# Recurrence of a hybrid trunk: a chunk's values formed beside the preceding chunk's solution, response products one gap earlier, VectorE's order changed

## Reference

```python
def rwkv_scan(s0, r, w, k, v, a_vec, b_vec, reverse, emit):
    def step(s, inp):
        r_t, w_t, k_t, v_t, a_t, b_t = inp
        sa = jnp.einsum('bhvk,bhk->bhv', s, a_t)
        s = s * w_t[:, :, None, :] + sa[..., None] * b_t[:, :, None, :] + v_t[..., None] * k_t[:, :, None, :]
        y = jnp.einsum('bhvk,bhk->bhv', s, r_t) if emit else None
        return s, y
...
for layer in range(2):
    m = token_mixer(modulate(rmsnorm(h)))    # windowed attention, rwkv7_bidirectional, differential attention
    h = h + mod * rmsnorm(m)
    f = swiglu(...) if layer == 0 else moe_swiglu(...)
    h = h + mod * rmsnorm(f)
```

## Time and profile before

| | |
|---|---|
| median of three runs | 2939.35 us |
| profiled execution, its time | 2935.08 us |
| its span | 2933.3 us |
| TensorE busy | 2817.0 us, 96% |
| VectorE, ScalarE busy | 1175.5 us (40%), 697.1 us (24%) |
| recurrence, seven chunks of layer 0 | 167.14 us |
| recurrence, seven chunks of layer 1 | 163.45 us |

### The profile page before, as it was taken

One profiled execution on the slowest core, in us unless ns is written; L12 is line 12 of the kernel. 1 busy time (PEld: TensorE's weight loads), 2 busy tenths in 40 slices (PEclk: granted clock), 3 DMA queues, 4 the chain that ended last, 5 costly groups with the idle time before them and its releaser, 6 DMA issues.

```text
span 2933.3 us, 61839 instructions
## 1 busy us (share of the span) xinstructions
PE 2817.0 (96%) x28070; PEld 1674.7 (57%) x28070; DVE 1175.5 (40%) x2420; ACT 697.1 (24%) x1449; POOL 3.0 (0%) x7
## 2 busy tenths in 40 slices
PE   8999899999999999999988999989999999999997
PEld 3467767445767888874478777873333333333332
DVE  4777565444646444237776454431011010111101
ACT  3345312444322111012454216620000000000000
POOL 0000000000000000000000000000000000000000
PEclk9999999999999999999999999999999999999998
DMA  7100134111332433232000442448999999999995
GB/s 289 58 3 4 34 128 150 44 65 58 115 108 93 144 115 88 79 119 83 30 4 4 152 158 87 151 174 335 416 359 375 408 362 386 392 364 413 364 379 198
DMA packets 188780, 534.44 MB, mean 182 GB/s; under 512 B 6112, under 2 KB 80096, under 8 KB 171104
## 3 DMA queue, kind: packets, MB, share of 16 engines
q1 hardware_dynamic: 187440, 526.21, 47.7%
q0 software_dynamic: 1072, 4.19, 0.4%
HBM read 528.29 MB, written 2.10 MB: 181 GB/s over the span
## 4 chain that ended last, share of the span: by engine, by line
PE 93%; DVE 4%; ACT 1%; issue 1%; DMA 1%; SPq 0%; DVEq 0%; ACTq 0%
PE bank L575 70%; PE bank L714 12%; PE bank L1355 8%; PE bank L833 2%; PE bank L1217 1%; DVE WR L2475 1%; DVE WR L2494 1%; DMA WR<-in_low_first 1%; ACT ar L1652 1%; DVE RS L2603 0%; ACT WR L1652 0%; DVE RS L2368 0%; PE bank L1524 0%; ACT L1652 0%; DVE HT L2280 0%
## 5 line engine op out<-in xcount | busy, mean ns | idle before, releaser
L1652 ACT ACTIVATE ar<-bank 128x256 f32<-128x256 f32 (+2 forms) x360 | 168.5, 471 | 1572.8 <-PE bank L575 1095.4
L575 PE MATMUL bank<-AT,WR 128*128 128x512 f32 (+1 forms) x1408 | 521.4, 520 | 5.7 <-ACT AT L1652 3.7
L575 PE MATMUL bank<-WR,ar 128*32 128x512 f32 (+1 forms) x4464 | 444.5, 555 | 1.6 <-DVE ar L2937 1.6
L575 PE MATMUL bank<-ar 128*32 128x512 f32 (+6 forms) x3990 | 431.2, 510 | 8.7 <-ACT ar L1652 5.9
L575 PEld LDWEIGHTS bank<-AT,WR 128*128 128x128 f32 x1408 | 262.5, 192 | 215.6 <-issue 201.0
L575 PEld LDWEIGHTS bank<-ar 128*32 128x32 f32 (+3 forms) x3990 | 176.3, 124 | 248.5 <-issue 237.4
L575 PEld LDWEIGHTS bank<-WR,ar 128*32 128x32 f32 x4464 | 143.7, 110 | 288.8 <-issue 285.8
L1652 ACT ACTIVATE WR<-bank 128x512 f32<-128x512 f32 (+1 forms) x224 | 122.9, 592 | 217.4 <-PE bank L575 183.7
L575 PE MATMUL bank<-AT,ar 128*32 128x512 f32 (+1 forms) x1456 | 151.8, 562 | 12.1 <-ACT AT L1652 12.1
L2947 DVE TENSOR_TENSOR YB<-YB,bank 128x512 f32<-128x512 f32 x28 | 18.0, 684 | 343.3 <-PE bank L575 343.3
L1652 ACT ACT_TABLE_LOAD x111 | 142.4, 1283 | 13.6 <-DVE ar L2329 7.8
(11 more groups left out here) (367 smaller groups left out, 3295.6 us busy)
## 6 DMA issues: line engine op xcount, KB each, us to landing
WR<-in_moe_w_down SPq DMA_DIRECT2D x27, 2048.0 KB, 15.5
WR<-in_ada_w SPq DMA_DIRECT2D x20, 2048.0 KB, 7.9
ar<-in_moe_w_down SPq DMA_DIRECT2D x20, 2048.0 KB, 14.7
WR<-in_w_in SPq DMA_DIRECT2D x18, 2048.0 KB, 9.1
WR<-in_moe_w_gate SPq DMA_DIRECT2D x18, 2048.0 KB, 17.2
WR<-in_moe_w_up SPq DMA_DIRECT2D x15, 2048.0 KB, 16.2
WR<-in_moe_w_up SPq DMA_DIRECT2D x18, 1536.0 KB, 7.7
WR<-in_moe_w_gate SPq DMA_DIRECT2D x15, 1536.0 KB, 9.0
```

Of the source, the lines that this page charges most:

```text
L575: return pe.matmul(o, lhsT, rhs, start=first, stop=last)
L1652: return act.activation(out, in_, func, **k)
```

## The change

On TensorE, `values_turned(i)` is split into `value_turned(i, q, h)` and issued inside `solve(i-1)`, two matmuls of the values behind each two of the solution; only chunk 0's values stay where they were. They signal a semaphore of their own, `values_full`, and their copies another, `values_in`, so that the ring `A` no longer counts them. In chunks 1 to 7 `against(i, 0)` moves ahead of level 2, `against(i, 2)` stands behind level 2, `against(i, 4)` behind `inverse_doubled(i, 2)` and `against(i, 6)` behind level 3; between `inverse_doubled(i, 3)` and level 4 stands nothing. Chunk 0 keeps its order. On ScalarE the values' copies keep their place and wait for `state(i-1)` as well. On VectorE `kept(0, 2)` stands ahead of `masked(2)` (behind it in chunk 0), `kept(2, 4)` behind `masked(2)`, `kept(4, 6)` ahead of `masked(3)` (chunk 0: behind it), `kept(6, 8)` behind `masked(3)` (chunk 0: ahead of `masked(4)`), `bonus_keys` behind `begin_inverse`.

```diff
--- before.py
+++ after.py
@@ -449,6 +449,7 @@
         inverse_ready, state_ready = sem("inverse_begun"), sem("state_ready")
         bonus_ready = sem("bonus_ready")
         uv_cleared = sem("state_rows_cleared")
+        values_full, values_in = sem("chunk_values_turned"), sem("chunk_values_in")
 
         chunks, expert_chunks, lent = [], [], []
@@ -861,15 +862,12 @@
                             if q == n + 1:
                                 last.then_inc(V_.full, 1)
 
-                def values_turned(i):
-                    for h in range(2):
-                        A.done(("vt", l, i, h))
-                    for q, h in hq:
-                        c = CH * (i if q < 4 else BWD[i])
-                        last = mm(two[h][64:128, 64 * q:64 * q + 64], Rv[64 * h:64 * h + 64, q % 4, c:c + CH],
-                                  eye[64 * h:64 * h + 64, 64 * h:64 * h + 64], True, True)
-                        if q == 7:
-                            last.then_inc(A.full, 1)
+                def value_turned(i, q, h):
+                    c = CH * (i if q < 4 else BWD[i])
+                    ins = mm(two[h][64:128, 64 * q:64 * q + 64], Rv[64 * h:64 * h + 64, q % 4, c:c + CH],
+                             eye[64 * h:64 * h + 64, 64 * h:64 * h + 64], True, True)
+                    if q == 7:
+                        ins.then_inc(values_full, 1)
 
                 def gram(i, what, bank, q, h):
                     ba, aa = BK[i % 2][64 * h:64 * h + 64, q, 0:64], pair(MV[:, i % 2, 0, :], q, h)
@@ -883,7 +881,7 @@
                     S.done(("T1", l, i, n))
                     if beside == "X":
                         pe.wait_ge(operands_ready, seen(operands_ready))
-                        pe.wait_ge(A.free, A.jobs[("vt", l, i, 1)])
+                        pe.wait_ge(values_in, 2 * (NCH * l + i) + 2)
                     if beside == "LT":
                         pe.wait_ge(S.free, S.jobs[("gram", l, i + 1, "X")])
                     for q in range(8):
@@ -953,10 +951,14 @@
                     pe.wait_ge(A.free, A.jobs[("XT", l, i, 4)])
                     for h in range(2):
                         A.done(("U", l, i, h))
-                    for q, h in hq:
-                        last = mm(two[h][0:64, 64 * q:64 * q + 64], pair(XT[1], q, 1 - h), pair(G, q, 1 - h), True, True)
-                        if q == 7:
-                            last.then_inc(A.full, 1)
+                    for q in range(8):
+                        for h in range(2):
+                            ins = mm(two[h][0:64, 64 * q:64 * q + 64], pair(XT[1], q, 1 - h), pair(G, q, 1 - h), True, True)
+                            if q == 7:
+                                ins.then_inc(A.full, 1)
+                        if i < NCH - 1:
+                            for h in range(2):
+                                value_turned(i + 1, q, h)
 
                 def y_of_chunk(i, bank):
                     pe.wait_ge(A.free, A.jobs[("U", l, i, 1)])
@@ -1008,7 +1010,8 @@
                 pe.wait_ge(responses_ready, seen(responses_ready))
                 against(0, 0)
                 pe.wait_ge(V_.free, V_.jobs[("v", l, 3)])
-                values_turned(0)
+                for q, h in hq:
+                    value_turned(0, q, h)
                 inverse_doubled(0, 2)
                 against(0, 2)
                 ybank = None
@@ -1021,18 +1024,22 @@
                         level(i, 1)
                         state(i - 1)
                         inverse_doubled(i, 1)
-                        values_turned(i)
                         if i <= 4:
                             bonus(i - 1)
-                        level(i, 2)
                         pe.wait_ge(responses_ready, seen(responses_ready))
                         against(i, 0)
+                        level(i, 2)
+                        against(i, 2)
                         inverse_doubled(i, 2)
-                        against(i, 2)
+                        against(i, 4)
                     level(i, 3, "X" if i < NCH - 1 else None)
-                    against(i, 4)
+                    if i == 0:
+                        against(i, 4)
+                    else:
+                        against(i, 6)
                     inverse_doubled(i, 3)
-                    against(i, 6)
+                    if i == 0:
+                        against(i, 6)
                     level(i, 4, "LT" if i < NCH - 1 else None)
                     if i == 0:
                         pe.wait_ge(uv_cleared, seen(uv_cleared))
@@ -1774,22 +1781,33 @@
                     act.wait_ge(A.full, A.taken)
                     free(f(x, bank, ACT.Copy))
 
-                def stacked_in(rows):
+                def halves_in(rows, h):
+                    bank = (banks[2], banks[7])[h]
+                    return f(UV[rows, :, h, :], bank[rows, :].rearrange("p (q w) -> p q w", q=8), ACT.Copy)
+
+                def solved_in():
 
                     for h in range(2):
                         A.take()
                         act.wait_ge(A.full, A.taken)
-                        bank = (banks[2], banks[7])[h]
-                        free(f(UV[rows, :, h, :], bank[rows, :].rearrange("p (q w) -> p q w", q=8), ACT.Copy))
+                        free(halves_in(slice(0, 64), h))
+
+                def values_kept(i):
+
+                    if i:
+                        act.wait_ge(V_.full, V_.jobs[("state", l, i - 1)])
+                    for h in range(2):
+                        act.wait_ge(values_full, 2 * (NCH * l + i) + h + 1)
+                        halves_in(slice(64, 128), h).then_inc(values_in, 1)
 
                 for d in range(2):
                     decays(l, 1, d)
                 for i in range(NCH):
                     if i:
-                        stacked_in(slice(0, 64))
+                        solved_in()
                     for n in range(5):
                         if n == 2:
-                            stacked_in(slice(64, 128))
+                            values_kept(i)
                         if n < 4:
                             copied(X[1], banks[0])
                         else:
@@ -2557,21 +2575,28 @@
                         state(i - 1)
                         if i <= 4:
                             bonus_out(i - 1)
+                        kept(i, 0, 2)
                     masked(2)
                     if i == 0:
                         v(dve.memset(UV[0:64, :, :, :], 0.0), uv_cleared, wait=False)
+                        kept(i, 0, 2)
+                    kept(i, 2, 4)
                     if i + 2 < NCH:
                         centre(l, i + 2)
-                    kept(i, 0, 2)
+                    if i:
+                        kept(i, 4, 6)
+                    masked(3)
+                    if i == 0:
+                        kept(i, 4, 6)
+                    else:
+                        kept(i, 6, 8)
+                    if i < NCH - 1:
+                        begin_inverse(i + 1)
                     if i < 4:
                         bonus_keys(l, i)
-                    masked(3)
-                    kept(i, 2, 4)
-                    if i < NCH - 1:
-                        begin_inverse(i + 1)
-                    kept(i, 4, 6)
+                    if i == 0:
+                        kept(i, 6, 8)
                     masked(4)
-                    kept(i, 6, 8)
                     if i < NCH - 1:
                         begin_turned(i + 1)
                     if i < 4:
```

## The result

Five runs of the changed kernel gave 2915.13 to 2922.68 us, median 2917.04; five runs of the kernel before in the same comparison 2935.08 to 2945.32, median 2938.74. The ratio is 0.9927, 95% interval 0.9913 to 0.9942: 21.7 us saved, where 28 were forecast. The forecast 2911 is 6 us too low; the range, 2899 to 2928, holds the time. The profiled execution took 2915.13 us with a span of 2913.3; against the 2933.3 of before the spans differ by 20.0 us.

The account below looks back on a forecast made before the run. TensorE, busy 96% of the span, was taken to bound the kernel; 13.2 + 22.3 + 11.5 - 12.2 - 1.6 = 33.2 us, less 5.6 for instruction supply, about 28 off 2939.35, gave 2911 us, range 2899 to 2928.

Parts of the forecast that it names:

- Part 1: Values inside solve, chunks 1 to 7: the moved matmuls cost nothing, 14 x 0.94 = 13.2 us off TensorE's path.
- Rival (b): Solve with values: the four quarters don't work side by side, 1.9 us, the 13.2 us stay; time 2924; chance 0.04.
- Part 2: TensorE's wait before against(i, 4) goes: 9.3 + 9.4 us, and 3.6 in chunk 0; sum 22.3 us.
- Part 3: TensorE's wait before from_state's second part goes: 5.2 + 4.3 = 9.5 us; with chunk 0, sum 11.5 us.
- Part 4: Costs of the new order: 12.2 us idle before level 4 and 1.6 us for a later masked(2).
- The bare gap: Between inverse product 3 and level 4: 0.76 us idle waiting for X(3), in 16 chunks, 12.2 us.
- ScalarE's thin margin: ScalarE before X(3)'s copies: needs 3.7 us of TensorE's 4.0, margin 0.3; half a microsecond over costs 8 us.
- `masked(2)` behind `kept`: VectorE in chunks without bonus: kept(i, 0, 2) delays masked(2) by about 0.4 us, 4 chunks, 1.6 us.
- Part 5: TensorE's instruction supply in denser runs: 0.4 us lost per chunk, 5.6 us; bounds nothing more and 20 us.
- rival (d): Supply runs out at nearly every one of six packets a chunk: 50 us against 33, time 2956; chance 0.06.
- (a): Both new dense runs on TensorE stall for instructions, 20 us instead of 5.6; gain 13, time 2926; chance 0.12.
- (c): Level, mask, product, copy chain binds, giving the waits' gains back: about 28 us, time 2935 to 2939; chance 0.08.

Follow-up runs that it names:

- e2: The changed kernel with the values again as a block of their own behind inverse product 1, so the new order alone: 2920.80 us, ratio 0.9933.
- e9: The changed kernel with extra matmul pairs that wait for nothing before chunk 0 (1024 in layer 0, 512 in layer 1): 2951.26 us, run once.
- e3: The changed kernel without the state's part of y in from_state, 32 pairs in eleven of fourteen chunks: 2910.69 us, ratio 0.9902.
- e12: The changed kernel with the values' matmuls beside the solution left out in chunks 1 to 7 of both layers: 2905.46 us, ratio 0.9888.
- e13: e11 with the values beside the solution instead of as a block of their own: 2911.78 us, ratio 0.9904.
- e10: e11 with the values transposed by 8 matmuls of 128x64 instead of 16 of 64x64: 2924.24 us, ratio 0.9960.
- e11: The kernel before with its TensorE order and values block, but VectorE's kept work ahead of masked(3) and masked(4): 2914.81 us, ratio 0.9917.

## Why the prediction was right in sign and 6 us too low

**Part 1**, the block: right as a block, wrong in what it brings. Solve with values, 64 records, takes 0.94 to 0.96 us in seven of the fourteen chunks and 1.1 to 1.3 in three; in the other four PE pauses inside it at a packet's end, and it takes 1.3 to 1.9 us (the one of the timeline above 1.5, from 279.46 to 280.96). Rival (b), quarters that don't work side by side, is refuted. The Trainium skill's rule in "TensorEngine Tiling (Array Packing)", "Gotcha 1: PSUM Pressure", which spoke for it, doesn't hold here: two row halves write two partition halves of one bank, 64 records in 0.94 us where two quarters take 0.94 for 32. But of the 13.2 us only 1.5 (the fourteen) to 3.8 (the medians) were paid out, change against e2.

**Part 2**: right. The waits of 9.3 + 9.4 us behind `kept` are down to one of 0.4. In chunk 0 PE's waits for DVE and ACT that belong to this are now:

```profile
PE bank L576 <- DVE ar L2347: 0.5, 1, 0.5
PE bank L576 <- ACT WR L1659: 0.5, 1, 0.5
PE bank L576 <- DVE WR L2493: 0.3, 1, 0.3
PE bank L576 <- DVE WR L2512: 0.2, 1, 0.2
```

0.2 us for `kept` where I left 0.4, and 0.3 for a mask.

**Part 3**: right. 5.2 + 4.3 us at `narrow` are gone, and chunk 0's 1.75 whole, where I took 1.0. The two chunks 0 gave 5.1 us; my terms for them, 3.6 + 2.0 less twice 0.76, came to 4.1.

**Part 4**: right. The bare gap is 5.1 us in seven in layer 0, 0.73 each, forecast 0.76; over both layers 10.4 us new against 10.6. But I charged it in 16 chunks, 12.2 us: chunk 0 keeps `against(i, 6)` before level 4, so the edit leaves 14 gaps bare, and the forecast should have been 1.5 us larger. ScalarE's thin margin held: the gap is 0.68 to 0.75 us in all fourteen chunks, and in chunk 5 ScalarE had stood idle 0.54 us when X(3) came. `masked(2)` behind `kept` costs less than I took: in the chunk shown, level 2 starts at 287.94 and `against(i, 2)`, at 289.12, gives way to product 2 at 290.09, 0.97 us instead of 0.85: 0.1 us, not 0.4.

**Part 5**: this is the step that failed, in size. I took 0.4 us a chunk, 5.6 in all, as the mean of nine gaps seen; measured are 13.6 us more of issue idle, 8.0 more than the term. A second shortfall is Part 1's: PE's busy time fell by 8.0 us, not by 13.2, so 5.2 less. Against that stand 1.0 us more from the two chunks 0, 1.6 for the mask, which stands in no wait of the fourteen, and 0.2 at the bare gap, less 0.4 for the one `kept` wait left: 27.6 - 8.0 - 5.2 + 1.0 + 1.6 + 0.2 - 0.4 = 16.8 for the recurrence, and 16.7 were measured there. Why the term was too small: I took gaps as events with a typical length, one or so a chunk, and didn't work out a rate of supply. The rows had what was needed for half of this: six packets a chunk, 128 pairs each, and blocks of 128 pairs in 1.9 us, denser than anything before. What they didn't have is the period of packets when PE takes them as fast as they come, 3.57 us; e9 gave it. Without Part 5 my forecast made a chunk 21.5 us (330.6 less 29.2, over 14); set against 744 pairs at 27.9 ns, 20.8 us, that leaves 0.7 us for every other wait, the bare gap of 0.76 among them, and a gain of 13 us by packing would have looked doubtful. My argument against rival (d), that a packet lasts 3.8 us at the pace of the sparse blocks, held: the supply runs out at 29 of the 81 packets of the fourteen, and the time didn't rise.

**The rivals.** (a), supply decides with 20 us instead of 5.6, priced at 2926: it is the same mechanism at a larger size, and the truth, 13.6, lies between its size and mine. That the outcome, 2917, is nearer to the forecast than to 2926 is in part luck: the recurrence gave 16.7 us where I had 27.6, 3.3 came from outside it, where I had counted nothing, and the medians differ by 1.7 more than the two traces do. (b) and (c) are refuted, (d) did not come about. The price of (b) should read 2925.

**What stays open:** the 3.3 us outside the recurrence; why the next packet's transfer starts only when PE is at work on the last one; how the two layers come to share the gains of e3 and e12 so unevenly; and why PE's busy time fell by 8.0 us where blocks of 13.2 went. The order alone (e2) raised it by 2.7 us against the kernel before. Some of the rest may lie in how a gap is counted, since a record's modelled end reaches some 0.2 us past the next start: from start to start the issue gaps rose by 17.8 us (6.5 to 24.3), not by 13.6.

## What to carry to other kernels

Where TensorE runs small matmuls in all four quarters, count pairs of weight load and matmul as a resource beside array time: here 27.9 ns each in an unbroken run and 31 in e13, against 15 ns of array time on four quarters and 29 on two. That is a guide to where work laid beside other work stops being free, not a price list: the same pairs took 317 to 322 us by the phase of the packets alone. In such a stretch leaving out pairs helped (e12), and merging them did not where it left half the array idle (e10). Before moving blocks on the bound engine, try the order of the engine that frees its buffers: VectorE's order alone (e11) gave all that the moved products gave (e2), and left no gap bare before level 4.

## What the runs showed of the hardware that I had not expected

- PE's instructions come in packets of 16 KB for 128 pairs. In an unbroken run one comes every 3.57 us (3.3 to 3.8), though the transfer takes 0.95 to 1.28 us: the next one starts 1.0 to 1.1 us after PE has gone on with the last, and its first instruction runs 2.3 to 2.7 us after that start.
- The waits for them carry no releaser; they are rows with "issue" inside a block, and their sum rose from 4.3 to 17.9 us when only the order and the packing changed, with the same 28070 matmuls.
- Sixteen records of 128x64 weights on 128 columns, all in one column half of the array, take 1.9 us, twice the time of 32 records of 64x64 over two quarters.
- Shifting all packet ends by 32 to 96 pairs moved the fourteen chunks by -1.6 to +3.3 us (one trace each): that much of a difference between two versions of such a kernel is neither's merit.
